# Two attention-mixing stages of a two-block network: gates as tanh of half the argument, third gate group ahead of the A branch's turn, dense groups ending with a step

## The reference

```
n = rms_norm_2(h, norm_g[i, 1])
(aq, ak, av, bq, ..., bgate, cq, ck, cv, ga, gb, gc) = split_cols(n @ w_in[i], IN_SPLITS)
ya = diff_attention(...)     # branch A, 8 score maps, then an RMS norm per head
yb = nsa_attention(...)      # branch B, 24 score maps, its three parts weighted by sigmoid(bgate)
yc = swa_sink_attention(...) # branch C, 8 score maps
merged = (sigmoid(ga) * (ya @ w_branch[i, 0]) + sigmoid(gb) * (yb @ w_branch[i, 1])
          + sigmoid(gc) * (yc @ w_branch[i, 2]))
h = h + merged @ w_out[i]
```

## Time and profile before

| what | value |
|---|---|
| median of 3 runs (lowest, highest) | 3397.63 us (3391.75, 3397.7) |
| the profiled execution's own time | 3395.16 us |
| its span, first to last instruction | 3393.0 us |
| PE busy | 3248.4 us, 96% of the span |
| DVE, ACT, POOL busy | 54%, 46%, 5% |
| granted TensorE clock, mean | 0.986 |
| mixing stages, step 0 to end | 2178 to 2436 us and 2900 to 3158 us |

### The profile page before, as it was taken

The page is one execution under the profiler, slowest core; times in us unless marked ns, Lnnn a source line. Parts: engine busy times, 40 slices in busy tenths (PEclk is TensorE's granted clock), DMA queues, the critical chain, the costliest instruction groups (busy, mean ns, idle before and its releaser), DMA issues.

```text
span 3393.0 us, 39683 instructions
## 1 busy us (share of the span) xinstructions
PE 3248.4 (96%) x16403; PEld 2721.6 (80%) x16403; DVE 1820.6 (54%) x2379; ACT 1561.8 (46%) x1949; POOL 182.6 (5%) x297
## 2 busy tenths in 40 slices
PE   8999999979999999999999999988999999988998
PEld 6888888867888888878888888876788788866886
DVE  4456455475454555554564554654645555645545
ACT  4444444354444434443444444575444544665434
POOL 0000000031000000030000000022000000121000
PEclk9999999989999999999999999999999999999999
DMA  6554555523555545565455555653455555634553
GB/s 207 190 167 166 191 176 196 185 94 118 188 195 189 182 146 182 186 205 186 162 174 187 175 197 187 172 157 95 157 186 168 176 190 176 180 103 121 183 187 111
DMA packets 324031, 576.23 MB, mean 170 GB/s; under 512 B 45385, under 2 KB 130460, under 8 KB 323724
## 3 DMA queue, kind: packets, MB, share of 16 engines
q1 hardware_dynamic: 321324, 566.71, 51.2%
q0 software_dynamic: 2384, 6.64, 0.8%
q10 hardware_dynamic: 144, 0.35, 0.0%
HBM read 571.53 MB, written 1.09 MB: 169 GB/s over the span
## 4 chain that ended last, share of the span: by engine, by line
PE 86%; DVE 6%; ACT 5%; issue 1%; DMA 1%; DVEq 0%; SPq 0%; ACTq 0%
PE up L1690 19%; PE up L1692 19%; PE up L1691 19%; PE acc L1690 8%; PE acc L1692 8%; PE acc L1691 8%; DVE w_lo L989 2%; ACT w_hi L577 2%; PE up L2008 1%; ACT units L721 1%; DVE xT_lo L1101 1%; PE acc L1787 1%; ACT xT_hi L642 0%; PE acc L2234 0%; PE up L2203 0%
## 5 line engine op out<-in xcount | busy, mean ns | idle before, releaser
L989 DVE TENSOR_TENSOR w_lo<-raw,w_hi 128x2048 fp32r<-128x2048 f32 x543 | 1234.5, 2275 | 1300.4 <-ACT w_hi L577 1295.2
L577 ACT ACTIVATE w_hi<-raw 128x2048 fp32r<-128x2048 f32 x543 | 1032.9, 1903 | 1375.7 <-PE up L1692 1014.8
L1690 PE MATMUL up<-w_hi,xT_hi 128*128 128x512 f32 (+1 forms) x2492 | 984.1, 395 | 55.4 <-DVE xT_lo L1101 18.7
L1692 PE MATMUL up<-w_hi,xT_lo 128*128 128x512 f32 (+1 forms) x2492 | 976.5, 392 | 0.0
L1691 PE MATMUL up<-w_lo,xT_hi 128*128 128x512 f32 (+1 forms) x2492 | 975.6, 391 | 0.0
L1690 PEld LDWEIGHTS up<-w_hi,xT_hi 128*128 128x128 f32 x2492 | 472.1, 189 | 161.0 <-issue 21.3
L1692 PEld LDWEIGHTS up<-w_hi,xT_lo 128*128 128x128 f32 x2492 | 472.3, 190 | 98.0
L1691 PEld LDWEIGHTS up<-w_lo,xT_hi 128*128 128x128 f32 x2492 | 472.7, 190 | 93.9
L1690 PE MATMUL acc<-w_hi,ff_hi 128*128 128x512 f32 x1216 | 480.8, 395 | 3.5 <-DVE ff_lo L1126 3.5
L1692 PE MATMUL acc<-w_hi,ff_lo 128*128 128x512 f32 x1216 | 474.2, 390 | 0.0
L1691 PE MATMUL acc<-w_lo,ff_hi 128*128 128x512 f32 x1216 | 473.6, 389 | 0.0
(11 more groups left out here) (299 smaller groups left out, 2249.9 us busy)
## 6 DMA issues: line engine op xcount, KB each, us to landing
raw<-in_ffn_down SPq DMA_DIRECT2D x88, 1024.0 KB, 4.8
raw<-in_ffn_gate SPq DMA_DIRECT2D x80, 1024.0 KB, 5.1
raw<-in_ffn_up SPq DMA_DIRECT2D x80, 1024.0 KB, 5.1
raw<-in_ffn_wi SPq DMA_DIRECT2D x80, 1024.0 KB, 5.0
raw<-in_ffn_wo SPq DMA_DIRECT2D x44, 1024.0 KB, 4.9
raw<-in_w_in SPq DMA_DIRECT2D x38, 1024.0 KB, 5.0
raw<-in_conv_w_in SPq DMA_DIRECT2D x24, 1024.0 KB, 5.2
raw<-in_w_in SPq DMA_DIRECT2D x44, 256.0 KB, 4.7
```

Of the source, the lines that this page charges most:

```text
L577: nc.scalar.activation(w_hi[n % RING][:, 0:c], raw[n % RING][:, 0:c], ACT.Copy).then_inc(hi_ready, 1)
L989: nc.vector.tensor_tensor(w_lo[n % RING][:, 0:c], raw[n % RING][:, 0:c], w_hi[n % RING][:, 0:c].bitcast(F32), ALU.subtract).then_inc(lo_re ...
L1690: pe.matmul(ps, lh, rh, start=start, stop=False)
L1692: return pe.matmul(ps, ll, rh, start=False, stop=stop)
```

## The change

Four edits, all in the mixing stages:

- The six gate groups and the small gate `gB` are evicted with Tanh of half the argument in place of Sigmoid. `half_rstd` (0.5 x `rstd`) is one more small DVE instruction behind `row_scale` of a mixing stage. Since sigmoid(z) is (1 + tanh(z/2))/2, `merge` multiplies by (gate + 1) in one `scalar_tensor_tensor` in place of a `tensor_tensor`, the sum is twice the reference's, and the residual addition takes 0.5 in place of 1.0. `gB` gets a DVE instruction that makes 0.5 x tanh + 0.5 of it, and POOL waits for DVE's eviction of `v` in place of ACT's.
- g2 stands before `ck` in the order of weight tiles, and before `ya0` and `ya1` in the order of work. `ck` follows `ya1`. The steps are now: g2 in 9 and 10; `ya0`, `ya1` in 11 (`YA_STEP` 11); `ck`, b0.0, b0.1 in 12; b1 in 13; g3 in 14 and 15; g4 in 16 and 17; g5 in 18 and 19; b2 in 20; b3.0 in 21; b3.1 in 22. Every group from g2 to g5, b0, b1 and b2 ends with a step.
- b0 takes bank 1 first and bank 0 second, in place of 0 and 1.
- Part p of a group waits for the holder of its own p-th bank only, in place of part 0 waiting for all holders.

```diff
+        half_rstd = rstd[:, NT:2 * NT]
...
-                for name in ("g0", "g1", "ck", "g2", "b0", "b1", "g3", "g4", "g5", "b2", "b3", "b4", "b5"):
+                for name in ("g0", "g1", "g2", "ck", "b0", "b1", "g3", "g4", "g5", "b2", "b3", "b4", "b5"):
...
-        YA_STEP = 9
+        YA_STEP = 11
...
-                   ("ck", "k", (0,), 0, 1), ("ya0", "", (0,), 0, 1), ("ya1", "", (1,), 0, 1),
-                   ("g2", "pair", (0, 1), 1, 0), ("b0", "b", (0, 1), 0, 1), ("b1", "b", (0, 1), 0, 1)]
+                   ("g2", "pair", (0, 1), 1, 0), ("ya0", "", (0,), 0, 1), ("ya1", "", (1,), 0, 1),
+                   ("ck", "k", (0,), 0, 1), ("b0", "b", (1, 0), 0, 1), ("b1", "b", (0, 1), 0, 1)]
...
-            BEFORE[name] = [holder[b] for b in in_banks if b in holder]
+            BEFORE[name] = [holder.get(b) for b in in_banks]
...
-        for j, piece in enumerate(parts_in("g0", "g1", "ck", "ya0", "ya1", "g2", "b0", "b1", "g3", "g4", "g5", "b2", "b3")):
+        for j, piece in enumerate(parts_in("g0", "g1", "g2", "ya0", "ya1")):
             PIECES.setdefault(5 + j // 2, []).append(piece)
+        PIECES[12] = parts_in("ck", "b0")
+        for j, piece in enumerate(parts_in("b1", "g3", "g4", "g5", "b2")):
+            PIECES.setdefault(13 + j // 2, []).append(piece)
+        PIECES[STEPS - 2], PIECES[STEPS - 1] = ([piece] for piece in parts_in("b3"))
...
-                            last = nc.scalar.activation(gB[:, t, :], up[t][:, 384:408], ACT.Sigmoid,
-                                                        scale=rstd[:, t:t + 1])
+                            last = nc.scalar.activation(gB[:, t, :], up[t][:, 384:408], ACT.Tanh,
+                                                        scale=half_rstd[:, t:t + 1])
...
-                            last = nc.scalar.activation(gates_of[int(name[1])][:, t, :], up[t][:], ACT.Sigmoid,
-                                                        scale=rstd[:, t:t + 1])
+                            last = nc.scalar.activation(gates_of[int(name[1])][:, t, :], up[t][:], ACT.Tanh,
+                                                        scale=half_rstd[:, t:t + 1])
...
+                if halved:
+                    step(nc.vector.tensor_scalar(half_rstd, rstd[:, 0:NT], 0.5, None, ALU.mult))
...
+                        nc.vector.tensor_scalar(gB, gB, 0.5, 0.5, ALU.mult, ALU.add)
...
-                        last = nc.vector.tensor_tensor(dst, gates_of[j][:, t, :], up[BANKS[f"b{j}"][t]][:], ALU.mult)
+                        last = nc.vector.scalar_tensor_tensor(dst, gates_of[j][:, t, :], 1.0, up[BANKS[f"b{j}"][t]][:],
+                                                              ALU.add, ALU.mult)
...
-                pending.append(1.0)
+                pending.append(0.5)
...
-                    if part == 0:
-                        for held in BEFORE[name]:
-                            evicted(held)
+                    if part < len(BEFORE[name]) and BEFORE[name][part]:
+                        evicted(BEFORE[name][part])
...
-                        pool.wait_ge(dense_act, ACT_IN * s[1] + EVICTED["v"][0])
+                        pool.wait_ge(dense_dve, DVE_IN * s[1] + EVICTED["v"][1])
```

More of the change, by code:

```diff
@@ L1113, in norm_xs, with row_scale @@
                 dve.wait_ge(ss_ready, seen.next(ss_ready, NT))
-                row_scale()
-            def row_scale():
+                row_scale(then == "mix")
+            def row_scale(halved=False):
                 v = nwv[:, 0:NT]
```

## The result

The changed kernel takes 3355.02 us (median of 4 runs, 3349.96 to 3358.16) against 3394.69 us (4 runs, 3391.34 to 3397.7). The ratio is 0.9878, 95% interval 0.9866 to 0.9889: about 1.2% faster. The profiled execution took 3349.96 us, its span is 3348.2 us, 44.8 us shorter than before.

The account below looks back on a forecast made before the run. PE, busy 96% of the span, bounds the kernel, so time comes only from its idle gaps or lowered clock. Gone 53.7 us, new 19.4, net -34.3 on 3395.2: 3361 us, range 3345 to 3378 (8 times in 10).

Parts of the forecast that it names:

- Group ends moved to step ends: Both mixing stages: PE's six waits at dense group ends, 20.4 us per stage, all go, 40.8 us.
- the per-bank waits: Group v in both stages: its 0.7 us wait for cmp's eviction goes, 1.4 us together.
- Step 11: New PE wait of about 4.9 us at pair 10's turn in step 12, after short step 11; 9.8 us over two stages.
- The same chain elsewhere: Steps 8, 17, 18, 19, 21: new waits of 0.2 to 1.2 us at turns, 2.6 us per stage, 5.2 together.
- Clock and what else hangs on a wait: PE's lowered clock after waits: 11.5 us won back over both stages, 4 us newly lost behind step 12's wait.
- Outside the stages: Only the half_rstd link in the chain before each stage's start was priced: 0.4 us lost for both.
- Tanh: ACT table loads: twelve before gate evictions go, those before exps fall from 19 to 7; hardly counted in the sum.
- Small terms: Merge costs nothing more; half_rstd adds 0.2 us at each stage's start; gB's extra 0.2 us lies under step 5's scores.
- there was a new wait: Rival that no new wait appears because POOL and DVE run ahead of the count: 3342 us, chance 0.15.
- it did not spread: Rival that the chain binds in most aligned steps, 1 us more in ten steps per stage: 3381 us, chance 0.16.
- the loads went: Rival that table loads stay because the compiler takes Tanh from another set: at most 3369 us, chance 0.05.
- nothing came near to slower: Rival that the same chain is long enough to outweigh the whole gain: 3400 us or more, chance 0.02.

Follow-up runs that it names:

- bank_waits_only: The kernel before with only the per-bank waits (each part of a group waits for its own bank's holder): 3384.85 us, ratio 0.9967.
- late_split: The changed kernel with the split of b1's tile moved behind ya1 in step 11, no longer ahead of that step's scores: 3342.76 us, ratio 0.9854.
- more_dve: The changed kernel with five extra VectorE multiplications into an unused tile ahead of the scores of step 11: 3360.96 us, ratio 0.9891.
- late_splits: The changed kernel with b1's split behind ya1, and those behind g3, g4, g5 moved behind steps 16, 18, 20's score and row-sum work: 3341.59 us, ratio 0.9849.

## Why the prediction held, and where its sizes were off

The forecast was 3361 us (range 3345 to 3378), the result 3355. The forecast took 34.3 us off the profiled time. The profiled span became 44.8 us shorter (it is the fastest of the four runs), and the medians differ by 39.7. The mechanism held, a long wait in step 12 included. Some sizes were off, nearly all to the same side.

- **Group ends moved to step ends.** Right: the six waits, 20.4 us per stage, are gone. But the credit for one of them was wrong. The 3.6 us of step 10 was a wait for ya1 that only the second part of g2 needs, and bank_waits_only removes it in the old order. My sum had 1.4 us for the per-bank waits; alone they are worth 12.3 us in the stages. The total was not hurt, since either edit removes that wait.
- **Step 11.** Right in place and cause (late_split, more_dve). The size was 4.9 us, measured 3.96. Counted from the step's start, POOL was done at 8.8 us (2295.46), not 9.2. And PE turned the pair's first unit in between, which took it from 2294.54 to 2295.52; the 4.9 us leave only 0.3 us for that. The row at the turn itself is 3.5 us, under the 4 to 6 that I had named. Over two stages the difference is 1.9 us.
- **The same chain elsewhere.** 2.6 us per stage forecast, 1.37 measured (0.23, 0.62 and 0.52 us in steps 18, 19 and 21; none in 8 and 17). 2.5 us over two stages. late_splits shows that two of the three come from the same order of split and scores.
- **Clock and what else hangs on a wait.** The forecast had 11.5 us won and 4 lost, 7.5 us net. The stages got shorter by 40.6 us, the listed waits by 31.3 (21.0 to 5.3 us each), so 9.3 us are in this term. PE's busy time at the lower level fell from 27.1 to 13.2 us. If half of it is lost (12 matmuls took 5.26 us there and 2.82 at full clock), the loss fell from 13.6 to 6.6 us, an estimate. So the clock gave back some 7.0 of the 9.3 us. Both the old loss (11.5) and the new one (4) were put too low by 2 to 3 us, and that the errors cancel is luck. The other 2.3 us may be that matmuls overlap at their ends, so that each wait costs a little more than its row; that is not shown.
- **Outside the stages** the forecast had 0.4 us lost, and the trace has 4.2 us less. The stretches at the lower clock account for most of it; no experiment was made on why they differ. It is in one profiled execution of each, and the medians differ by 39.7 us, close to the stages' 40.6, so this part is best taken as chance.
- **Tanh.** The loads at L721 went from 19 to 7 and the twelve before evictions are gone, as forecast: no load stands between Exp and Tanh. The Trainium skill ("ScalarE: Activation LUTs", section "Table sets: the hidden batching unit") lists tanh in exp's set, and the trace agrees. The forecast that the loads hardly count in the new order held (0.9 us in the stages), and so did the one that they cost time in steps 16 and 18 of the old one (12 us with the clock).
- **Small terms.** `half_rstd` lengthened the wait at the start from 0.24 to 0.47 us, 0.2 us more as forecast. The new merge takes 684 ns as before.

The rivals fell: there was a new wait, it did not spread, the loads went, and nothing came near to slower.

## What to carry to other kernels

Let a group that must be moved out end just before work that needs none of its buffers: the eviction is then free. But what refills buffers must not stand ahead of the next scores in the same queues, least of all before a short step: late_split moves one split, by a condition of one line on ACT and one on DVE, and took 7.7 us off the stages, a fifth of what the whole change did. Edits that remove the same waits don't add: in the stages the table edit was worth 12 us alone and about 1 us beside the new order, the per-bank waits 12 and 3 (by the medians 10 and 3, 11 and 5). So price an edit in the order in which it will run, and look first for the wait condition that is wider than the data it guards.

## What the runs showed that was not expected

The clock fell behind short waits, and not each time: in late_split, 0.99 and 0.43 us of wait a microsecond apart in step 12 are followed by a granted clock of 0.56 over 7 us in the first stage, and by full clock in the second, with the same waits. In the kernel before, the 2.89 us wait of step 16 leaves it up in the first stage and is followed by 0.67 over the next 12 matmuls in the second. In the changed kernel the lower level ends 5.8 us after the 3.52 us wait in the first stage and 7.6 us after it in the second. So what the same wait costs in clock differs by 1 to 3 us from stage to stage, and nothing in the rows read here says which it will be.

POOL, the last link of the chain, takes nearly twice as long for the same 128x256 values when it multiplies by the row sum alone, as in branch C, as when it multiplies by a gate too (trace of before):

```profile
L2376 POOL TENSOR_SCALAR units<-units,rsum 128x256 f32<-128x256 f32 x40 | 42.5, 1062 | 214.3 <-DVE rsum L1247 214.2
...
L2376 POOL TENSOR_SCALAR units<-units,rsum,arena 128x256 f32<-128x256 f32 x32 | 17.9, 560 | 114.2 <-DVE rsum L1247 114.2
```

The instruction with fewer operands is the slower one, in durations that are rough on this engine. Whether branch C would gain from the other form, with a second factor of 1, was not tried.
